# Gathers of two expert tables issued two and two instead of one and one, from expert 33 on

## The chip, the core and the metric

The kernel runs on one core of one Trainium2 chip. Its time is the device time of one execution in microseconds (us). Work is spread over five engines that run their own instruction streams and meet only at semaphores: TensorE (PE, matmuls), VectorE (DVE), ScalarE (ACT), GpSimd (POOL) and SyncE (SP). Transfers run on 16 DMA engines; GpSimd issues the ones that this case is about.

## The reference, cut to what matters

Two transformer blocks follow each other. The change lies in the expert layer of the first one, in which each of 256 tokens picks 8 x 16 = 128 experts out of 16384, and each expert is one row of 1024 numbers in each of two tables:

```
def expert_chunk(args):                      # 128 tokens a chunk
    xc, ic, gc = args
    u = jnp.take(u_tab, ic, axis=0)          # rows of the first table
    a = jnp.einsum('chkd,cd->chk', u, xc)    # one dot a token and expert
    wgt = gc * jax.nn.gelu(a)
    vv = jnp.take(v_tab, ic, axis=0)         # rows of the second table
    return jnp.einsum('chk,chkd->cd', wgt, vv)
```

## The kernel before

The 256 tokens are two tiles of 128; a token is a partition. "Expert e" in the code is one of 128 places of a tile: e from 0 to 127 is the first tile, 128 to 255 the second. For each e GpSimd issues one indirect DMA that fetches for each of 128 tokens its own row of the first table (`gather_u`, L687, 128 rows of 4 KB, 512 KB) and one of the second table (`gather_v`, L701, as large). So there are 512 gathers, which land in a buffer of 12 slots of 1024 numbers a partition: `NU` = 5 slots for the first table and `NV` = 7 for the second.

What uses them, in this order for each e:

- VectorE multiplies the row of the first table with the token and sums (L2489), and then counts the semaphore `dot_ready` up (L2491). Between these dots it also does pieces of the routing that finds the next experts.
- ScalarE makes the weight of the expert from the dot (L1737, L1741) and spreads it on a diagonal 128x128 matrix (L1746), of which there are 8 places.
- TensorE multiplies the diagonal with the row of the second table and adds to a sum in PSUM (L1143; two matmuls, which the profile shows as four records). After every odd e it counts `pair_summed` up. Between the sums it does matmuls of the next layers and of the routing (L780, L1069 and others), whose results ScalarE copies out of PSUM (L1563).

GpSimd's stream is written out by hand and is in order: an instruction that waits holds all behind it. `gather_u(e)` waits until the dot of e-5 is done, since it overwrites that slot. `gather_v(e)` waits until the pair that holds e-7 is summed: with pairs counted after odd e, an odd e asks for the sum of e-6, and the even e behind it asks for the same count again. So only odd e can really wait there. At a few e `gather_u` also waits for the routing's indices (`idx_ready`), at multiples of 32 in the part that the change touches. Before, the order is u(e+1), v(e), u(e+2), v(e+1) and so on. SyncE streams the weights of the later layers (2 MB a piece) over its own queue at the same time, in parts of this stage.

Of the kernel before, what the change touches and what calls it, by code (L numbers as in the profile page):

```python
# [27 lines left out]
TT = SEQ // P  # L28
# [44 lines left out]
ROUTE = 2 * TOPK  # L73
EXPERTS = HEADS * TOPK
# [170 lines left out]
def pairs(experts):  # L245

    return (experts + 1) // 2


def build(nc, T, out):  # L250

    with ExitStack() as ctx:
# [195 lines left out]
        def flag(name):  # L448

            if name not in S_:  # L450
                S_[name] = sem(name)
            return S_[name]

        def group_wait(eng, name, i):
            g = (name, i)
            eng.wait_ge(bank_full[GROUP_BANK[g]], GROUP_USE[g] + 1)
# [52 lines left out]
        def turn_wait(eng, *u):  # L509

            eng.wait_ge(turned, turn_no[u] + 1)
# [22 lines left out]
        def summed_wait(eng, t):  # L534

            eng.wait_ge(flag("pair_summed"), pairs(EXPERTS * (t + 1)))
# [5 lines left out]
        def route_step(e):  # L542

            return e // TOPK if e < ROUTE else e // ROUTE + 1
# [7 lines left out]
        def _(sp):  # L552
            second_halves = []
            for c, (_, w, k0, kt, col, n) in enumerate(CHUNKS):
                b = BEFORE[c]
                if c == FRONT:
# [79 lines left out]
        def _(pool):  # L636
# [41 lines left out]
            def gather_u(e):  # L678

                r, k, slot = e // ROUTE, e % ROUTE, e % NU  # L680
                if e in FIRST_IDX:
                    pool.wait_ge(flag("idx_ready"), FIRST_IDX.index(e) + 1)
                elif e == TOPK or (k == 0 and r):
                    pool.wait_ge(flag("idx_ready"), route_step(e) + len(FIRST_IDX))
                if e >= NU:
                    pool.wait_ge(flag("dot_ready"), e - NU + 1)
                pool.indirect_dma_start(  # L687
                    u_rows[:, slot, :], None, T["peer_u"],
                    bass.IndirectOffsetOnAxis(ap=expert_idx[:, r % 2, k:k + 1], axis=0),
                ).then_inc(u_full[slot], 16)  # L690

            def gather_v(e):

                r, k, slot = e // ROUTE, e % ROUTE, e % NV
                if e >= NV:
                    pool.wait_ge(flag("pair_summed"), pairs(e - NV + 1))
                if e == 0:
                    turn_wait(pool, "m", 1, 0)
                if e == 3:
                    group_wait(pool, "out1", 1)  # L700
                pool.indirect_dma_start(  # L701
                    v_rows[:, slot, :], None, T["peer_v"],
                    bass.IndirectOffsetOnAxis(ap=expert_idx[:, r % 2, k:k + 1], axis=0),
                ).then_inc(v_full[slot], 16)
# [1 line left out]
            gather_u(0)  # L706
            gather_v(0)
            gather_u(1)
            for e in range(1, TT * EXPERTS):
                if e + 1 < TT * EXPERTS:  # L710
                    gather_u(e + 1)
                gather_v(e)

            summed_wait(pool, TT - 1)
            pool.wait_ge(flag("dot_ready"), TT * EXPERTS)
# [2465 lines left out]
```

## Time and profile before

| | |
|---|---|
| median of 3 runs | 1384.9 us (1382.9 to 1387.51) |
| profiled execution, first to last instruction | 1366.9 us |
| first gather issued, last sum of experts | 152 us, 914 us |
| gathers | 512 of 512 KB |
| GpSimd busy | 500.2 us |

The profile gives the span of the profiled execution and not a time of its own that takes in what lies around it; median less span is 18.0 us, which is the start and the end of a run as far as this shows. Over half of the span is the expert stage. Its rows are read from GpSimd's timeline (when a gather is issued, and how long GpSimd sat idle before it), from the DMA share and rate in stretches of time, and from the count of matmuls that TensorE had begun by then. A gather's record on GpSimd is only the issue; the transfer runs later.

### The profile page before, as it was taken

Reading aid. Unit: us, or ns where it says so; the run is one execution under the profiler, and the core shown is the slowest. Engines: PE = TensorE matmul, PEld = TensorE weight load, DVE = VectorE, ACT = ScalarE, POOL = GpSimd, SP = SyncE. Lnnn points to the kernel's source line nnn. Section 1 sums busy time; section 2 is a strip of 40 time slices with the busy share of each in tenths; the row PEclk is TensorE's granted clock in tenths of the full one; section 3 lists DMA queues with packets and bytes.
Section 4 is the critical chain, followed back from the end, with each engine's and each line's share of the span. In section 5 each row is a group of like instructions: output and inputs, shape, how many; then the busy total and the mean of one; then the engine's idle time right before and its main releaser. Section 6 shows DMA issues by size and latency. Waiting matters only on the chain. (4 is left out here: it accounts for less than half of the span.)

```text
span 1366.9 us, 14592 instructions
## 1 busy us (share of the span) xinstructions
PE 1199.9 (88%) x4663; PEld 665.4 (49%) x4663; DVE 861.8 (63%) x1765; ACT 420.2 (31%) x1138; POOL 500.2 (37%) x580
## 2 busy tenths in 40 slices
PE   7899888888778978876788889789999999999997
PEld 4676554433344542222345433236544545999443
DVE  2657669574663654776746557679989543676345
ACT  2213334344223343343423324432323311222000
POOL 1000356666665666766666666630000000000000
PEclk9999999999998999999999999999999999999999
DMA  9998789999998999999999999986644444454450
GB/s 358 390 349 326 286 319 339 367 357 367 364 366 300 406 403 405 407 377 364 340 371 353 400 405 409 377 306 233 224 139 148 145 150 156 157 175 145 175 184 31
DMA packets 134303, 405.66 MB, mean 297 GB/s; under 512 B 10153, under 2 KB 11585, under 8 KB 133971
## 3 DMA queue, kind: packets, MB, share of 16 engines
q0 software_dynamic: 75024, 273.19, 53.1%
q1 hardware_dynamic: 57860, 127.48, 25.8%
q10 hardware_dynamic: 1342, 4.06, 0.8%
q8 instruction: 38, 0.62, 0.2%
q14 instruction: 39, 0.31, 0.1%
HBM read 403.12 MB, written 1.05 MB: 296 GB/s over the span
## 5 line engine op out<-in xcount | busy, mean ns | idle before, releaser
L1143 PE MATMUL psum<-gathered,modr 128*128 128x512 f32 x1024 | 505.0, 633 | 130.3 <-DMA gathered<-in_peer_v_dram,expert_idx 49.0
L2489 DVE CUSTOM_DVE_ANT_0 gathered<-gathered,psum 128x1024 f32<-128x1024 f32 x256 | 311.5, 1217 | 202.3 <-DMA gathered<-in_peer_u_dram,expert_idx 153.3
L1143 PEld LDWEIGHTS psum<-gathered,modr 128*128 128x128 f32 x1024 | 190.7, 199 | 404.7 <-issue 284.9
L687 POOL DMA_INDIRECT gathered<-in_peer_u_dram,expert_idx x256 | 244.9, 957 | 240.5 <-DVE expert_idx L1997 144.0
L701 POOL DMA_INDIRECT gathered<-in_peer_v_dram,expert_idx x256 | 242.6, 947 | 169.9 <-remote 73.7
L780 PE MATMUL psum<-featT,weight_ring 128*128 128x128 f32 (+2 forms) x960 | 145.3, 305 | 14.4 <-issue 11.3
L780 PEld LDWEIGHTS psum<-featT,weight_ring 128*128 128x128 f32 x960 | 133.7, 196 | 43.9 <-issue 35.6
L780 PE MATMUL psum<-weight_ring,featT 128*128 128x512 f32 x336 | 147.9, 596 | 1.3 <-ACT featT L1563 0.8
L1737 ACT ACTIVATE gel<-dots 128x1 f32<-128x1 f32 x256 | 51.1, 200 | 255.1 <-issue 128.1
L1746 ACT ACTIVATE modr<-ident,wgt 128x128 f32<-128x128 f32 x256 | 102.8, 402 | 18.5 <-issue 1.1
L780 PEld LDWEIGHTS psum<-weight_ring,featT 128*128 128x128 f32 x336 | 62.6, 190 | 78.8 <-issue 76.6
L1741 ACT ACTIVATE wgt<-gel,expert_gate 128x1 f32<-128x1 f32 x256 | 75.4, 294 | 17.9 <-issue 0.3
L1989 DVE TENSOR_TENSOR work<-work 128x1088 f32<-128x1088 f32 (+5 forms) x87 | 68.6, 801 | 9.6 <-issue 2.8
L725 POOL DMA_DIRECT2D gathered<-in_b_in_dram x6 | 5.3, 942 | 138.6 <-ACT gathered L1585 104.2
L1585 ACT COPY work<-psum 128x128 f32<-128x128 f32 x32 | 8.4, 262 | 81.5 <-remote 44.6
L1978 ACT ACTIVATE work<-work,pack 128x256 f32<-128x256 f32 x28 | 12.7, 500 | 56.8 <-DVE work L1989 56.8
L1989 DVE TENSOR_TENSOR vectors<-weight_ring 128x1024 f32<-128x1024 f32 x14 | 16.5, 1220 | 20.9 <-PE psum L1512 20.9
L1563 ACT COPY featT<-psum 128x512 f32<-128x512 f32 (+1 forms) x24 | 12.4, 554 | 55.0 <-PE psum L752 53.8
L780 PE MATMUL psum<-weight_ring,uT 128*128 128x512 f32 x64 | 28.2, 593 | 1.0 <-ACT gathered L1585 1.0
L1989 DVE TENSOR_TENSOR gathered<-gathered,psum 128x256 f32<-128x256 f32 (+1 forms) x17 | 8.6, 511 | 29.8 <-PE psum L780 24.9
L1473 PE MATMUL psum<-featT,weight_ring 128*128 128x128 f32 x224 | 27.3, 275 | 0.0
L1473 PEld LDWEIGHTS psum<-featT,weight_ring 128*128 128x128 f32 x224 | 26.1, 192 | 0.0
(443 smaller groups left out, 1343.1 us busy)
## 6 DMA issues: line engine op xcount, KB each, us to landing
weight_ring<-in_w_in_dram SPq DMA_DIRECT2D x16, 2048.0 KB
weight_ring<-in_w_up_dram SPq DMA_DIRECT2D x8, 2048.0 KB
weight_ring<-in_w_down_dram SPq DMA_DIRECT2D x8, 2048.0 KB
weight_ring<-in_ada_w_dram SPq DMA_DIRECT2D x5, 2048.0 KB
work<-in_ada_w_dram SPq DMA_DIRECT2D x5, 2048.0 KB, 16.3
weight_ring<-in_peer_wq_dram SPq DMA_DIRECT2D x3, 2048.0 KB
gathered<-in_ada_w_dram SPq DMA_DIRECT2D x2, 2048.0 KB, 14.5
gathered<-in_peer_u_dram,expert_idx POOLq DMA_INDIRECT x256
```

What stands on the lines that cost most here:

```text
L687: pool.indirect_dma_start(u_rows[:, slot, :], None, T["peer_u"], bass.IndirectOffsetOnAxis(ap=expert_idx[:, r % 2, k:k + 1], axis=0),).the ...
L701: pool.indirect_dma_start(v_rows[:, slot, :], None, T["peer_v"], bass.IndirectOffsetOnAxis(ap=expert_idx[:, r % 2, k:k + 1], axis=0),).the ...
L780: last = pe.matmul(psum[0:m, bank, 0:n], lhs(k), rhs(k), start=(k == 0), stop=(k == kt - 1))
L1143: mm = pe.matmul(psum[:, SUM_BANK + half, :], diag[:, e % 8, :], v_rows[:, slot, 512 * half:512 * (half + 1)], start=(e % EXPERTS == 0), s ...
L1473: last = pe.matmul(psum[:, UP_BANKS * (n % 2) + bank, at:at + P], a(g, m), b(g), start=(g == 0), stop=(g == 3))
L1563: ins = act.activation(dst, src, func, **kw) if func else act.copy(dst, src)
L1737: act.activation(gel[:, col:col + 1], dots[:, col:col + 1], ACT.Gelu_apprx_tanh)
L1741: act.activation(wgt[:, col:col + 1], gel[:, col:col + 1], ACT.Copy, scale=expert_gate[:, r % 2, k:k + 1])
L1746: act.activation(diag[:, e % 8, :], ident[:, :], ACT.Copy, scale=wgt[:, col:col + 1]).then_inc(flag("diag_full"), 1)
L1978: act.activation(ffT[:, k, :], ffT[:, k, :], ACT.Relu, bias=pk("b_up")[:, k:k + 1])
L1989: return dve.tensor_tensor(o, a, b, op)
L2489: dve.tensor_tensor_reduce(u_rows[:, slot, :], u_rows[:, slot, :], h2_rows[t], 1.0, 0.0, ALU.mult, ALU.add, dots[:, col:col + 1])
```

## The change

GpSimd's loop is left as it was up to e = 32. From e = 33 it goes in steps of two and issues u(e+1), u(e+2), v(e), v(e+1). The waits inside `gather_u` and `gather_v` and all other engines are untouched.

```
             gather_u(0)
             gather_v(0)
             gather_u(1)
-            for e in range(1, TT * EXPERTS):
-                if e + 1 < TT * EXPERTS:
-                    gather_u(e + 1)
+            for e in range(1, ROUTE + 1):
+                gather_u(e + 1)
                 gather_v(e)
+            for e in range(ROUTE + 1, TT * EXPERTS, 2):
+                for ahead in (e + 1, e + 2):
+                    if ahead < TT * EXPERTS:
+                        gather_u(ahead)
+                for now in (e, e + 1):
+                    if now < TT * EXPERTS:
+                        gather_v(now)
```

`ROUTE` is 32, `TT * EXPERTS` 256. On GpSimd, around the place where the new loop starts (the first row is u(32); u is L687 and v is L701), this stood before:

```order
L687 DMA gathered<-in_peer_u_dram,expert_idx 128x1024 [waits dot_ready,idx_ready]
L701 DMA gathered<-in_peer_v_dram,expert_idx 128x1024 [waits pair_summed]
L687 DMA gathered<-in_peer_u_dram,expert_idx 128x1024 [waits dot_ready]
L701 DMA gathered<-in_peer_v_dram,expert_idx 128x1024 [waits pair_summed]
L687 DMA gathered<-in_peer_u_dram,expert_idx 128x1024 [waits dot_ready]
L701 DMA gathered<-in_peer_v_dram,expert_idx 128x1024 [waits pair_summed]
L687 DMA gathered<-in_peer_u_dram,expert_idx 128x1024 [waits dot_ready]
L701 DMA gathered<-in_peer_v_dram,expert_idx 128x1024 [waits pair_summed]
```

And this stands there now:

```order
L687 DMA gathered<-in_peer_u_dram,expert_idx 128x1024 [waits dot_ready,idx_ready]
L701 DMA gathered<-in_peer_v_dram,expert_idx 128x1024 [waits pair_summed]
L687 DMA gathered<-in_peer_u_dram,expert_idx 128x1024 [waits dot_ready]
L701 DMA gathered<-in_peer_v_dram,expert_idx 128x1024 [waits pair_summed]
L687 DMA gathered<-in_peer_u_dram,expert_idx 128x1024 [waits dot_ready] x2
L701 DMA gathered<-in_peer_v_dram,expert_idx 128x1024 [waits pair_summed] x2
L687 DMA gathered<-in_peer_u_dram,expert_idx 128x1024 [waits dot_ready] x2
L701 DMA gathered<-in_peer_v_dram,expert_idx 128x1024 [waits pair_summed] x2
```

In each block of four only the two in the middle have changed places: u(e+2) stands one place earlier, ahead of v(e) with e odd, and v(e) one place later. This happens 111 times, for e = 33, 35, ... 253.

At the end of GpSimd's part of this stage (gathers of experts 254 and 255), this stood before:

```order
L701 DMA gathered<-in_peer_v_dram,expert_idx 128x1024 [waits pair_summed]
L687 DMA gathered<-in_peer_u_dram,expert_idx 128x1024 [waits dot_ready]
L701 DMA gathered<-in_peer_v_dram,expert_idx 128x1024 [waits pair_summed] x2
L718 DMA gathered<-xres 128x1024 [waits bank_free6,bank_free7,dot_ready,pair_summed]
```

And this stands there now:

```order
L687 DMA gathered<-in_peer_u_dram,expert_idx 128x1024 [waits dot_ready] x2
L701 DMA gathered<-in_peer_v_dram,expert_idx 128x1024 [waits pair_summed] x3
L724 DMA gathered<-xres 128x1024 [waits bank_free6,bank_free7,dot_ready,pair_summed]
```

The last gather of all is v(255) in both, in the same place.

## Rows read from the trace of the kernel before

**Rows 1.** The page: the span, and the whole of it in 40 equal slices

```profile
span 1366.9 us, 14592 instructions
...
DMA  9998789999998999999999999986644444454450
GB/s 358 390 349 326 286 319 339 367 357 367 364 366 300 406 403 405 407 377 364 340 371 353 400 405 409 377 306 233 224 139 148 145 150 156 157 175 145 175 184 31
```

**Rows 2.** The page: groups of the expert stage (busy, mean; idle before, what ended it)

```profile
L1143 PE MATMUL psum<-gathered,modr 128*128 128x512 f32 x1024 | 505.0, 633 | 130.3 <-DMA gathered<-in_peer_v_dram,expert_idx 49.0
L2489 DVE CUSTOM_DVE_ANT_0 gathered<-gathered,psum 128x1024 f32<-128x1024 f32 x256 | 311.5, 1217 | 202.3 <-DMA gathered<-in_peer_u_dram,expert_idx 153.3
...
L687 POOL DMA_INDIRECT gathered<-in_peer_u_dram,expert_idx x256 | 244.9, 957 | 240.5 <-DVE expert_idx L1997 144.0
L701 POOL DMA_INDIRECT gathered<-in_peer_v_dram,expert_idx x256 | 242.6, 947 | 169.9 <-remote 73.7
```

**Rows 3.** Stretches of 60 us (busy of PE, PEld, DVE, ACT, POOL; clock, DMA, GB/s)

```profile
320.00:380.00 60.00, 47.41 (x131) 21.90 (x132) 36.40 (x96) 20.19 (x68) 38.34 (x41) 0.94 0.97 362
...
500.00:560.00 60.00, 47.47 (x102) 17.49 (x103) 33.92 (x75) 22.17 (x70) 39.65 (x42) 0.97 1.03 406
```

**Rows 4.** GpSimd's timeline around one stop (start, length; idle before, releaser)

```profile
345.00 0.94 POOL L687 DMA_INDIRECT gathered<-in_peer_u_dram,expert_idx  x1 [0.30 <-issue]
349.51 0.94 POOL L701 DMA_INDIRECT gathered<-in_peer_v_dram,expert_idx  x1 [3.56 <-remote]
350.75 0.94 POOL L687 DMA_INDIRECT gathered<-in_peer_u_dram,expert_idx  x1 [0.30 <-issue]
```

**Rows 5.** GpSimd's timeline: the stop before and the stop behind that one

```profile
326.33 0.94 POOL L701 DMA_INDIRECT gathered<-in_peer_v_dram,expert_idx  x1 [3.23 <-remote]
...
372.63 0.94 POOL L701 DMA_INDIRECT gathered<-in_peer_v_dram,expert_idx  x1 [3.38 <-remote]
```

**Rows 6.** Stretches of 2 us, before and behind the stop at 349 us

```profile
344.00:346.00 2.00, 1.43 (x4) 0.49 (x3) 1.18 (x2) 0.62 (x3) 1.64 (x2) 1.00 1.04 422
...
350.00:352.00 2.00, 1.63 (x4) 0.68 (x4) 1.88 (x9) 0.77 (x3) 1.39 (x3) 1.00 0.66 156
```

**Rows 7.** Groups from 150 us to 345.9 (PE) and 345.98 (POOL)

```profile
L1143 PE MATMUL psum<-gathered,modr 128*128 128x512 f32 x250 | 125.0, 642 | 29.6 <-issue 17.0 <-ACT modr L1746 9.0 <-DMA gathered<-in_peer_v_dram,expert_idx 3.6
...
L701 POOL DMA_INDIRECT gathered<-in_peer_v_dram,expert_idx x65 | 62.3, 959 | 41.8 <-issue 16.2 <-remote 13.1 <-PE psum L1143 12.5
```

**Rows 8.** Timelines of TensorE and ScalarE at the stop at 326, TensorE before 349

```profile
322.18 1.05 PE L1069 MATMUL psum<-work 128*128 128x128 f32 x8
...
326.28 0.59 ACT L1563 COPY work<-psum 128x512 f32<-128x512 f32 x1 [4.90 <-remote]
...
338.32 3.81 PE L1143 MATMUL psum<-gathered,modr 128*128 128x512 f32 x8
```

**Rows 9.** Another stop: GpSimd's timeline, and groups from 150 to 457.3 us

```profile
456.34 0.94 POOL L687 DMA_INDIRECT gathered<-in_peer_u_dram,expert_idx  x1 [0.30 <-issue]
459.38 0.94 POOL L701 DMA_INDIRECT gathered<-in_peer_v_dram,expert_idx  x1 [2.10 <-remote]
...
L1143 PE MATMUL psum<-gathered,modr 128*128 128x512 f32 x384 | 191.5, 641 | 51.7 <-ACT modr L1746 23.6 <-issue 19.6 <-DMA gathered<-in_peer_v_dram,expert_idx 8.5
...
L701 POOL DMA_INDIRECT gathered<-in_peer_v_dram,expert_idx x101 | 96.3, 954 | 74.3 <-remote 27.8 <-issue 25.0 <-PE psum L1143 21.6
```

**Rows 10.** Waits before gathers, 254 to 906 us: L701 (two rows), L687 (one)

```profile
  remote: 70.4, 27
...
  PE psum L1143: 19.6, 8
...
  DVEq L2491: 17.7, 23
```

**Rows 11.** The chain that ended last: from the last gather's issue to its landing

```profile
904.90 7.71 DMA gathered<-in_peer_v_dram,expert_idx
```

**Rows 12.** GpSimd's timeline: a gather of the first table that waits

```profile
504.31 1.32 POOL L687 DMA_INDIRECT gathered<-in_peer_u_dram,expert_idx  x1 [1.90 <-DVEq L2491]
```

## The prediction

> **What bounds the kernel now.** I read the page first. The DMA share stands at 9 tenths or near it from the start of the expert stage to its end, and the rate in its slices moves between about 300 and 409 GB/s [rows 1]. The groups of the stage say the same from the side of the users: VectorE's dots stood idle mostly because a row of the first table had not landed (153.3 us), TensorE's sums because one of the second had not (49.0 us, the rest in weight loads) [rows 2]. So the stage is paced by gathers. Who paces the gathers differs by stretch, and that is the second view. From 500 to 560 us the share is 1.03 at 406 GB/s, the most that this stage shows for long: the transfers themselves are the bound. From 320 to 380 us it is 0.97 at 362 GB/s [rows 3]. Of the 19 slices that lie within the changed part (slices 8 to 26), 7 have 400 or more and 12 have less, 358.6 on average [rows 1]. Were those 12 raised to 405, they would give back 12 x 34.2 us x (1 - 358.6 / 405) = 47 us. That is a ceiling for anything that a better order of gathers can bring.
>
> What keeps the 12 lower is in GpSimd's timeline, the third view. Between stops it issues a gather each 1.24 us (0.94 and 0.30 behind it), which at 512 KB is 423 GB/s, more than the 409 of the best slice. Then, at a gather of the second table, it stops for 3.56 us [rows 4], and so it did 23.2 us earlier and does 23.1 us later, for 3.23 and 3.38 us [rows 5]: 16 gathers at 1.24 and one stop of 3.3, which is 8 experts in 23.2 us. The stop reaches the transfers: before it the share is 1.04 at 422 GB/s, right behind it 0.66 at 156 [rows 6].
>
> Why does it stop? The fourth view is a count. By 345.98 us GpSimd had issued 65 gathers of the second table, so the one that waits is v(65), which asks for the pair of experts 58 and 59. By 345.9 TensorE had begun 250 records of sums, at four an expert: experts 0 to 61 are done, and the one asked for lies in the row that ends at 342.1 [rows 7, 8]. The count was due 7 us or more before GpSimd saw it. ScalarE shows the same at the stop before: the scores that it copies were made by 323.23, and it is let go at 326.28, after 4.90 us of waiting, within 0.1 us of GpSimd [rows 5, 8]. So what TensorE has done comes late to whoever waits, and to several at once. At another stop, before v(101), the needed count is of experts 0 to 95; with 384 records begun by 457.28 their sums were only just made, and yet GpSimd waits only 2.10 us [rows 9]. Seen from TensorE's end the counts are late by over 7 us in one case and by about 2 in the other; seen from GpSimd's last issue (345.94, 457.28) they come 3.6 and 2.1 us later. The time since GpSimd fell still is what the cases share.
>
> **The change part by part.** Nothing is added or removed: 512 gathers, the same bytes, the same waits. In 111 blocks u(e+2) goes ahead of v(e), e odd, and each moves by one place, 1.24 us.
>
> - At a stop (v(e) waits, e odd): before, u(e+2) stood behind the wait; now it is issued first. There are 35 such stops in the changed part, 70.4 + 19.6 = 90.0 us in all, 2.6 each with the regular 0.30 in it [rows 10]. What this is worth hangs on what ends a stop. If it ends some time after GpSimd has fallen still, GpSimd now falls still 1.24 us later, the stop ends 1.24 us later and is as long as before: 16 gathers and 3.3 us for 8 experts, 23.2 us again, worth 0. If it ends at an instant that TensorE alone sets, the moved gather fills 1.24 us of it. I take the first, for what the two stops above share. The second is the lower bound in time, priced with the rivals.
> - Between stops: v(e) is issued 1.24 us later, lands later, and its sum is later by as much. But v(e+6), which asks for that sum, is moved back too (e+6 is odd). The loop of the second table has the same slack; v(e+1) keeps its place. Worth 0.
> - The first table: u(e+2) asks for the dot of e-3, now 9 issues behind that row's own gather (11.2 us) and not 10 (12.4). Where gathers land in some 7.7 us, as the last one does [rows 11], a dot of 1.22 us still ends before. Where weights share the engines it does not always: GpSimd waited for dots 23 times, 17.7 us in all [rows 10], as before u(117) for 1.90 us [rows 12]. These waits get longer for odd e and now hold up v(e) too. But there the share is 1.03 [rows 3], and the queue of issued gathers is what the engines work on; a later issue shortens the queue and not the rate. Worth 0 while it holds several gathers; the price without that cover is the second rival.
> - VectorE gets its rows two at a time, then none for two gathers. A dot is 1.22 us and the pace 2.9 us an expert [rows 2, 5], so the second of a pair waits no longer than it came early. Worth 0.
> - The end: v(255) keeps its place, and its landing is what the chain passes through [rows 11]. Worth 0.
>
> Sum: 0. The page's span stays at 1366.9 us, and with the 18.0 us by which the median exceeds it the time is 1384.9; I say 1384.
>
> Two rules of the Trainium skill bear on this. By "TensorE: Matmul & The Clock Gate" (The cost: per-tile semaphore tail) a matmul's increment is an event of tens of ns, about 25 + 26 ns for one; ScalarE's 3 us between the end of the scores and its release [rows 8] do not agree with it. By that rule a count would come at TensorE's instant, whatever GpSimd does, which is the second case of a stop, the first rival. The other speaks against any gain: "DMA: Bandwidth & Descriptors" (Where 436 GB/s comes from) has about 358 GB/s a core as what HBM gives. By it the 362 of 320 to 380 us would be the ceiling and the sum 0 for good; the 406 in the same stage [rows 3] does not agree, so I keep the 47 us as the ceiling.
>
> **The rivals.**
>
> 1. Faster: a stop ends at TensorE's instant, and each stop in a stretch below 400 GB/s is cut by 1.24 us. 12 of 19 slices have 35 x 12 / 19 = 22 stops: 27 us, 1358; with all 35, 43 us, 1342, which is close to the ceiling. For it: a semaphore has no reason to wait for GpSimd. Against it: the stops of 3.23, 3.56 and 3.38 us are nearly equal, though TensorE's work between them is not, and two waiters were let go together.
> 2. Slower: the wait of u(e+2) for a dot takes the place of the wait that is left. It sits in the stretches with weight traffic. The 23 waits, each 1.24 us longer, are 29 us, 1413, if nothing covers them; it decides when the queue of issued gathers runs dry, which by the 7.7 us from issue to landing [rows 11] takes a wait of about six gathers' issue. With a third of it uncovered, 1394.
> 3. The stops fall elsewhere. The order within a stop is new, so the counts that are seen at its end can be a pair more or a pair less, and a stretch can have a stop more or fewer. At 3.3 us each, two or three of them are 7 to 10 us to either side, 1375 to 1394.
>
> **How the numbers follow.** Unchanged cycle: 0.60, of which I give a bit over half to a time within 0.3% (4.2 us, about what this measurement can tell from no change), and the rest to both sides evenly by the third rival: 0.34 same, 0.13 faster, 0.13 slower. First rival 0.27, all faster. Second rival 0.13, all slower. So 0.40 faster, 0.34 same, 0.26 slower. The likeliest case has 1375 to 1394 for itself. The range reaches to the 1358 of the first rival, which leaves out the part of it beyond, and to 1397 on the other side, past the 1394 of the second.
>
> **What would show it.** Right: in the changed kernel's timeline stops before odd v stay 3.2 to 3.6 us long in the stretches below 400 GB/s, 8 experts keep to 23 us, and the last gather is issued near 905 us. First rival: stops of about 2.2 us, 8 experts in 22, the last issue near 878. Second: waits of L687 for VectorE's count well over 17.7 us, and a DMA share under 1.0 in the stretch 500 to 560. What would make the forecast wrong above all is that a stop is ended neither by GpSimd's stillness nor by TensorE, but by the queue of gathers itself: then one more gather in that queue could lengthen every stop, or one more count could slip through and remove some.

## The result, and the profile of the changed kernel

| | before | after |
|---|---|---|
| median, 20 executions each | 1380.5 us (1367.2 to 1387.5) | 1383.9 us (1378.7 to 1390.6) |
| profiled execution | span 1366.9 us [rows 1] | span 1380.0 us, its own time 1381.8 us |
| last gather issued | 904.90 us [rows 11] | 914.15 us |
| ratio after / before | | 1.0044, 95% interval 1.0023 to 1.0066 |

The change makes the kernel slower, by 0.44% or 6.1 us (0.0044 x 1380.5). The interval does not hold 1, though its lower end, 0.23%, lies under the 0.3% that this measurement can just tell from no change. The ratio compares only undisturbed executions taken beside each other on a chip, so it is not the quotient of the two medians. Of the executions of before, 8 of 20 are under 1376 us; of the changed kernel none is under 1378.7. The profile of before [rows 1] was one of those quick executions, so the 13.1 us between the two spans are not the price of the change.

The page of the changed kernel: span, DMA share and rate in 40 slices, the groups of the expert stage (all lines behind the loop are 6 higher).

```profile
span 1380.0 us, 14592 instructions
...
DMA  9999779999999999999999999986744534444450
GB/s 358 390 350 329 288 268 337 371 356 363 355 359 356 404 404 405 350 344 368 364 362 348 398 404 408 350 323 213 244 133 142 152 121 162 174 157 153 180 182 31
...
L1149 PE MATMUL psum<-gathered,modr 128*128 128x512 f32 x1024 | 513.0, 648 | 139.6 <-ACT modr L1752 65.8
L2495 DVE CUSTOM_DVE_ANT_0 gathered<-gathered,psum 128x1024 f32<-128x1024 f32 x256 | 311.0, 1215 | 201.5 <-DMA gathered<-in_peer_u_dram,expert_idx 151.6
...
L687 POOL DMA_INDIRECT gathered<-in_peer_u_dram,expert_idx x256 | 245.2, 958 | 246.6 <-DVE expert_idx L2003 143.8
L701 POOL DMA_INDIRECT gathered<-in_peer_v_dram,expert_idx x256 | 243.5, 951 | 171.8 <-remote 67.8
```

Against [rows 1] most slices move by a few GB/s in either direction, some by far more: the 13th has 356 where before had 300, the 6th, which ends ahead of the change, 268 where it had 319. Two neighbours fall together, the 17th and 18th (552 to 621 us): 350 and 344, where before had 407 and 377. And TensorE's sums, which had waited most for rows of the second table (49.0 us, [rows 2]), now wait most for ScalarE's diagonal (65.8 us).

The waits before gathers between 254 and 930 us, L701 (two rows) and L687 (one), in us and times. `remote` is a count that came when no instruction that sends it had just ended; `DVEq` is VectorE's count of dots:

```profile
  remote: 66.5, 27
...
  PE psum L1149: 23.7, 15
...
  DVEq L2497: 22.4, 21
```

At gathers of the second table GpSimd sat idle for 90.2 us, where it was 90.0 [rows 10]. The waits of the first table for a dot rose from 17.7 to 22.4 us. Three stops in GpSimd's timeline (start, length; idle before, releaser), with the gathers ahead of them:

```profile
369.68 0.94 POOL L687 DMA_INDIRECT gathered<-in_peer_u_dram,expert_idx  x1 [0.30 <-issue]
373.10 1.35 POOL L701 DMA_INDIRECT gathered<-in_peer_v_dram,expert_idx  x1 [2.48 <-remote]
...
387.20 0.94 POOL L687 DMA_INDIRECT gathered<-in_peer_u_dram,expert_idx  x1 [0.30 <-issue]
390.92 0.94 POOL L701 DMA_INDIRECT gathered<-in_peer_v_dram,expert_idx  x1 [2.77 <-PE psum L1149]
...
547.25 0.94 POOL L701 DMA_INDIRECT gathered<-in_peer_v_dram,expert_idx  x1 [2.23 <-remote]
```

The second gather of the pair is now issued ahead of the stop, and the stop is still 2.2 to 2.8 us here. That is less than the 3.2 to 3.6 us of [rows 4, 5], but before has such stops too (2.10 us in [rows 9]). Of all stops over 0.5 us from expert 33 on, the 67 in two profiles of before average 2.65 us, the 65 in two of the changed kernel 2.63 (the second profile of each belongs to the repeats below). Last, three stretches (busy of PE, PEld, DVE, ACT, POOL; clock, DMA share, GB/s) of after:

```profile
320.00:380.00 60.00, 51.84 (x161) 25.92 (x160) 37.55 (x94) 22.93 (x74) 39.04 (x42) 0.94 0.95 359
500.00:560.00 60.00, 46.45 (x91) 17.09 (x89) 27.50 (x57) 18.80 (x60) 35.63 (x38) 0.89 1.03 405
560.00:600.00 40.00, 32.06 (x67) 12.37 (x68) 30.98 (x82) 16.95 (x51) 26.72 (x28) 0.96 0.91 338
```

and the third of them in the kernel before:

```profile
560.00:600.00 40.00, 32.41 (x63) 12.20 (x62) 28.62 (x71) 16.95 (x51) 26.31 (x28) 0.87 0.99 379
```

The first two answer to [rows 3] and have hardly moved. The third is new to this document: the share falls from 0.99 to 0.91 and the rate from 379 to 338 GB/s.

### The profile page after: what moved, and what is told of

Same layout as the page of the kernel before. It is cut to its first block, busy times and chain, and to the rows that moved or that the text cites. A ratio compares the mean times of both kernels' runs of the same rounds, so it can differ in the third digit from the quotient of the medians.

```text
span 1380.0 us, 14592 instructions
## 1 busy us (share of the span) xinstructions
PE 1207.1 (87%) x4663; PEld 675.1 (49%) x4663; DVE 858.2 (62%) x1765; ACT 416.2 (30%) x1138; POOL 501.4 (36%) x580
## 4 chain that ended last, share of the span: by engine, by line
PE 43%; POOL 12%; issue 10%; DVE 9%; another core or an unknown queue 9%; DMA 8%; ACT 4%; DVEq 2%; ACTq 1%; POOLq 0%; SPq 0%
PE psum L786 18%; PE psum L1479 6%; POOL gathered L701 6%; PE psum L1518 6%; POOL gathered L687 6%; PE psum L1149 6%; DMA gathered<-in_peer_u_dram,expert_idx 5%; DVE gathered L2495 3%; ACT modr L1752 1%; DVEq L2497 1%; DMA work<-in_ada_w_dram 1%; DMA weight_ring<-in_w_in_dram 1%; DMA gathered<-in_peer_v_dram,expert_idx 1%; PE psum L879 1%
## 5 line engine op out<-in xcount | busy, mean ns | idle before, releaser
L1149 PE MATMUL psum<-gathered,modr 128*128 128x512 f32 x1024 | 513.0, 648 | 139.6 <-ACT modr L1752 65.8
L1149 PEld LDWEIGHTS psum<-gathered,modr 128*128 128x128 f32 x1024 | 201.1, 206 | 411.3 <-issue 354.0
L687 POOL DMA_INDIRECT gathered<-in_peer_u_dram,expert_idx x256 | 245.2, 958 | 246.6 <-DVE expert_idx L2003 143.8
L701 POOL DMA_INDIRECT gathered<-in_peer_v_dram,expert_idx x256 | 243.5, 951 | 171.8 <-remote 67.8
L1995 DVE TENSOR_TENSOR work<-work 128x1088 f32<-128x1088 f32 (+5 forms) x87 | 68.7, 803 | 12.2 <-issue 5.8
L1995 DVE TENSOR_TENSOR vectors<-weight_ring 128x1024 f32<-128x1024 f32 x14 | 16.5, 1219 | 20.9 <-PE psum L1518 20.9
L1995 DVE TENSOR_TENSOR gathered<-gathered,psum 128x256 f32<-128x256 f32 (+1 forms) x17 | 8.6, 511 | 29.8 <-PE psum L786 24.9
```

Of the source, the lines that this page charges most:

```text
L687: pool.indirect_dma_start(u_rows[:, slot, :], None, T["peer_u"], bass.IndirectOffsetOnAxis(ap=expert_idx[:, r % 2, k:k + 1], axis=0),).the ...
L701: pool.indirect_dma_start(v_rows[:, slot, :], None, T["peer_v"], bass.IndirectOffsetOnAxis(ap=expert_idx[:, r % 2, k:k + 1], axis=0),).the ...
L1149: mm = pe.matmul(psum[:, SUM_BANK + half, :], diag[:, e % 8, :], v_rows[:, slot, 512 * half:512 * (half + 1)], start=(e % EXPERTS == 0), s ...
L1995: return dve.tensor_tensor(o, a, b, op)
```

## The experiments

Two theories went in. Theory A: a stop ends some time after GpSimd has fallen still, whatever the order, and the loss comes from where the stops now fall. Theory B, the second rival of the prediction: a gather of the first table asks for its dot one place sooner, and that wait is the loss. Below, "asks n behind" means that a gather stands n issues behind the gather whose dot or sum it waits for; these counts come from the issue order, not from a trace. All ratios are to the kernel before, run beside the experiment.

**Where a pair begins.** The same pairs one expert later, from e = 34 (the edit is shown against the changed kernel), so that the gather which is moved past v(e) is another.

```
-            for e in range(1, ROUTE + 1):
+            for e in range(1, ROUTE + 2):
...
-            for e in range(ROUTE + 1, TT * EXPERTS, 2):
+            for e in range(ROUTE + 2, TT * EXPERTS, 2):
```

> The pairs begin at e = 34: v(e) with e even moves one place back, and it never asks for a new count; odd v and the waits of odd v keep their place, even u(e+2) asks for its dot one place sooner. Theory A (a stop at odd v ends some 3 us after GpSimd's last issue, and the loss comes from moving the gather that stops): stops at odd v as in the kernel before, 8 experts apart in the stretches below 400 GB/s, time that of before within 0.3%. Theory B (the loss comes from gathers of the first table that ask for a dot one place sooner): as slow as the changed kernel, +0.4%, with waits of L687 for VectorE over 20 us.

Measured: 1378.9 us, ratio 1.0016 (0.9989 to 1.0042). Not told apart from either kernel. GpSimd waited 24.5 us for dots and 96.6 us for sums (from 240 us on), so neither wait went away.

**One place sooner without pairs.** u(e+2) ahead of v(e), one and one.

```
-            for e in range(1, TT * EXPERTS):
-                if e + 1 < TT * EXPERTS:
-                    gather_u(e + 1)
+            for e in range(1, ROUTE + 1):
+                gather_u(e + 1)
+                gather_v(e)
+            gather_u(ROUTE + 2)
+            for e in range(ROUTE + 1, TT * EXPERTS):
+                if e + 2 < TT * EXPERTS:
+                    gather_u(e + 2)
                 gather_v(e)
```

> From expert 33 on one and one again, but every u(e+2) goes ahead of v(e): the move of the change for odd and even e alike. Theory A: the set of gathers at a stop is that of the changed kernel, so stops of about 2.9 us and 6 to 8 experts between them, +0.3 to +0.7%. Theory B: twice as many gathers ask sooner, so twice the loss, +0.8% or more, and waits of L687 for VectorE near 30 us.

Measured: 1380.6 us, 1.0023 (0.9996 to 1.0050). What was put there for theory B counted wrongly: one and one, every first-table gather still asks 10 behind, so this order does not double the demand. Only its place against the second table changes, which comes back below.

**Fewer buffers for the first table.** The order of before, `NU = 4`, `NV = 8`: every dot is asked for 8 behind.

```
-NU = 5
-NV = 7
+NU = 4
+NV = 8
```

> The order of before, with 4 slots for the first table and 8 for the second. The second table's gathers have one expert more of room before they stop, the first table's ask for a dot one expert sooner. Theory A: about 10 experts between stops of 3.3 us where it was 8, some 5 of 35 stops fewer, -15 to -20 us (-1.2%), unless the dot waits eat it. Theory B: dot waits rule, +1% or more, L687 waits for VectorE well over 40 us.

Measured: 1386.8 us, 1.0077 (1.0049 to 1.0105). Waits for dots 38.3 us, for sums 73.2 (from 240 us on). The 15 to 20 us that theory A hoped for did not come, and a shorter demand on dots costs by itself, with no pair anywhere.

**A throttle on the first table.** Five buffers, order of before, but each u(e) from e = 33 waits for the dot of e-3, 6 behind.

```
-                    pool.wait_ge(flag("dot_ready"), e - NU + 1)
+                    pool.wait_ge(flag("dot_ready"), e - NU + (3 if e > ROUTE else 1))
```

> The order of before; from expert 33 a gather of the first table waits for the dot of e-3 and not e-5, so that GpSimd can't run far ahead and is still for short times all along. Theory A: the counts come through in these short pauses, the stops at odd v vanish or fall under 1.5 us, and the time falls by 10 to 40 us in spite of the waits. Rival (counts come at an instant that TensorE sets, stillness or not): the stops stay and the new waits add to them, +20 us or more.

Measured: 1394.6 us, 1.0135 (1.0086 to 1.0184). The waits of L687, and then of L701, from 254 us on:

```profile
  DVEq L2491: 55.6, 39
...
  remote: 37.6, 17
...
  PE psum L1143: 19.1, 14
```

Theory A had this kernel 10 to 40 us faster, and it is slower. Waits for dots tripled and waits for sums fell from 90.0 to 56.7 us. So a part of such waits is only exchanged: when GpSimd stands before a dot, the late counts of sums come in meanwhile. 37.9 us more here and 33.3 us less there do not add up to the 19 us that were lost (0.0135 x 1380), so idle time of GpSimd is not lost time one for one.

**Both kernels again,** unchanged, as a measure of the spread.

> The kernel before, unchanged, as a second profiled execution and as a measure of what a comparison on one chip shows of no change: ratio 1.000 within 0.25%. Of GpSimd's idle time from expert 33 on, the first profile has 13 us before gathers of the first table and 81 us before those of the second, beyond the regular 0.30. If executions repeat, these stand again within 2 us each; if they do not, differences of some us between two profiles say nothing of a change.

> The changed kernel, unchanged, beside the same runs of before: +0.2 to +0.7%, as before. Theory A (stops at odd v last as long as before and only their places move): idle time before gathers of the second table as in the kernel before, 75 to 85 us. Theory B (the moved gathers of the first table wait for dots): idle time before gathers of the first table above that of before_again by 4 us or more, as 19 against 13 in the first profiles.

Measured: 0.9998 (0.9971 to 1.0026) and 1.0042 (1.0017 to 1.0067). The loss is real and repeats. The waits do so less well: after_again had 29.1 us for dots and 77.0 for sums, before_again 17.5 and 87.4. Differences of some us in the waits of one profile decide nothing alone.

**One and one around the change of tiles only** (e = 113 to 144), pairs elsewhere.

```
+            for e in range(33, 113, 2):
...
+            for e in range(113, 145):
...
+            for e in range(145, 256, 2):
```

> Pairs as in the changed kernel, but one and one for e from 113 to 144, where the second tile begins: there u(135) has to wait for the dot of 130, which waits until the first tile's sum is read, and in pairs v(133) and v(134) stand behind it. If the loss sits there (4.6 us of waiting at that place in the profile of the changed kernel, none in that of before): within 0.2% of before. If it is spread over the stage: 0.3% or more above it.

Measured: 1.0039 (1.0014 to 1.0063). Most of the loss stays, which is what was expected of a loss that is spread over the stage and not of one that sits at this place. Its profile says more, below.

**Threes,** three gathers of each table in turn: dots asked for 8, 11 and 11 behind.

```
+            for e in range(ROUTE + 1, TT * EXPERTS, 3):
+                for ahead in (e + 1, e + 2, e + 3):
...
+                for now in (e, e + 1, e + 2):
```

> Three and three in place of two and two: in a block the third gather of the first table asks for its dot 8 issues (10.0 us) behind that row's own gather, where pairs have 9 and one and one has 10. Theory B (dot waits): idle time before the first table's gathers 30 us or more, time +0.8% or more. Theory A (only the places of the stops): +0.2 to +0.6%, idle time before the first table's gathers as in pairs, near 20 us.

Measured: 1.0118 (1.0087 to 1.0150), nearly three times the loss of pairs. That makes threes the better probe of a place: the next three put them in parts of the stage only.

**Threes where dots were waited for** (e = 90 to 149 and 210 to 248), **threes elsewhere** (33 to 89 and 150 to 209), **threes at the end** (from 249), and **pairs with the last seven experts one and one.**

```
+            for e in range(90, 150, 3):
...
+            for e in range(210, 249, 3):
```

> Three first-table gathers and then three second-table ones, for experts 90 to 149 and 210 to 248 only; one and one elsewhere, the last seven experts included. In these stretches first-table gathers waited for dots in the traces so far (19.1 us in all with pairs, 25.8 with threes). All threes cost a ratio of 1.0118. Theory B (the earlier demand for a dot costs): 1.007 to 1.010. Theory A (only where the stops fall counts, which is as likely anywhere): about half of what all threes cost, 1.004 to 1.006. If the end costs most: 1.000 to 1.003.

```
+            for e in range(33, 90, 3):
...
+            for e in range(150, 210, 3):
```

> Threes for experts 33 to 89 and 150 to 209 only, where the traces so far show nearly no wait for a dot; one and one elsewhere. Theory B: 0.999 to 1.002. Theory A: 1.004 to 1.006.

```
+            for e in range(249, TT * EXPERTS, 3):
```

> Threes for experts 249 to 255 only. In the traces so far the sums that TensorE still had to do behind GpSimd's last gather took 11.3 us with threes, 9.6 with pairs and 8.4 to 8.8 with one and one. If the end costs only that: a ratio of 1.002 (2.5 to 2.9 us). If the end is what costs in threes: 1.006 or more. If it costs nothing: 1.000.

```
+            for e in range(33, 249, 2):
...
+            for e in range(249, 256):
```

> The pairs of the change for experts 33 to 248, one and one for the last seven. The change cost 1.0044. If the end takes about 1 us of it: 1.0035. If the end takes all: 1.000. If the end takes none: 1.0044.

Measured, in this order: 1.0100 (1.0060 to 1.0141), 1.0047 (1.0017 to 1.0076), 0.9995 (0.9967 to 1.0023), 1.0064 (1.0029 to 1.0099). The end costs nothing, in threes or pairs. The busy stretches cost about what theory B gave, the calm ones more than it gave and just what theory A gave. So B is right on where most of it is, and does not hold for all of it.

**Pairs that ask for nothing sooner.** Six buffers for each table, and TensorE counts every sum. In this setting every gather asks exactly 12 behind, in any of the three orders: pairs and threes still bunch two and three gathers, dots and sums, but no wait is nearer than with one and one. The lines that place the sixth slot among the twelve are left out of the edit.

```
-NU = 5
-NV = 7
+NU = 6
+NV = 6
...
-    return (experts + 1) // 2
+    return experts
...
-                if e % 2:
-                    mm.then_inc(flag("pair_summed"), 1)
+                mm.then_inc(flag("pair_summed"), 1)
```

> The order of the kernel before, with six row buffers for each table in place of five and seven, and TensorE counting every sum instead of every second. Now each gather of either table stands 12 issues behind the gather whose dot or sum it asks for (before: 10 for the first table, 12 and 14 in turn for the second). This is the base of the next two kernels. Dots should be waited for for under 4 us where it was 13, sums for somewhat more than the 81 us of before. The time: a ratio of 0.995 to 1.010.

```
+            for e in range(33, 256, 2):
```

> The pairs of the change on top of the six buffers. Counted out, all gathers still stand 12 issues behind the one they ask for: pairs bunch the gathers of a table and ask for nothing sooner (with five and seven buffers they asked for a dot 9 and 11 issues behind in turn). Theory B (the earlier demand for a dot costs): the same time as six_one, within 0.2%, and the waits for dots as in six_one. The rival (the bunching of two sums or two dots costs, whatever is asked): the pairs' 0.4% to 0.6% again, on top of six_one.

```
+            for e in range(33, TT * EXPERTS, 3):
```

> Three and three on top of the six buffers; all gathers again 12 issues behind what they ask for. Theory B: the time of six_one within 0.3%. The rival (bunching): some 1.2% over six_one, as three and three cost with five and seven buffers.

Measured: one and one 0.9946 (0.9923 to 0.9969), pairs 0.9936 (0.9910 to 0.9962), threes 0.9969 (0.9949 to 0.9988). On top of six buffers the pairs cost nothing (0.9936 / 0.9946 = 0.9990), and threes 0.23% in place of 1.18%. Bunching as such is not what costs. The waits of six_one (L687, then L701) and of six_pairs:

```profile
  DVEq L2490: 2.7, 9
...
  remote: 51.7, 21
  PE psum L1143: 50.9, 34
```

```profile
  DVEq L2497: 12.3, 22
...
  PE psum L1150: 56.0, 38
  remote: 38.4, 19
```

The pairs do raise the waits for dots (2.7 to 12.3 us; theory B had them equal, which was wrong), and those for sums fall by 8.2: an exchange, with nothing lost. All three beat both kernels; six_one and six_pairs are 0.5 to 0.6% faster than before (0.995 to 1.010 was expected of six_one).

**The demand brought back.** Six buffers, but a first-table gather waits for the dot of e-5, as with five: 10 behind one and one, 9 and 11 in pairs (the edit is shown against the six-buffer kernels). And five and seven buffers with every sum counted.

```
-                if e >= NU:
-                    pool.wait_ge(flag("dot_ready"), e - NU + 1)
+                if e >= 5:
+                    pool.wait_ge(flag("dot_ready"), e - 4)
```

> six_one with one line changed: a gather of the first table waits for the dot of e-5, as with five buffers, though it has a sixth. So it asks 10 issues behind again, and nothing else differs. This is the base of the next kernel. Theory B: waits for dots rise from 2.7 us towards the 17.5 of before, and the time by 0 to 0.3% over six_one (a ratio of 0.995 to 0.998 to before).

> six_pairs with the same line changed: the first gather of a pair asks for its dot 11 issues behind, the second 9, as in the change; sums are asked for 12 behind, as in six_pairs. Theory B (the dot asked for 9 behind is what costs): 0.3% to 0.7% slower than ask5_one and than six_pairs. The rival (with six buffers it was the second table's new spacing that made the pairs free, not the first table's): the time of ask5_one, within 0.2%.

```
-    return (experts + 1) // 2
+    return experts
...
-                if e % 2:
-                    mm.then_inc(flag("pair_summed"), 1)
+                mm.then_inc(flag("pair_summed"), 1)
```

> The kernel before (five and seven buffers, one and one) with TensorE counting every sum, so that a second-table gather asks for a sum 14 issues behind at every expert, where it was 12 and 14 in turn. If the counting is what gains in six_one: a ratio of 0.993 to 0.997. If the sixth buffer of the first table gains it: 0.999 to 1.001.

Measured: ask5_one 0.9999 (0.9965 to 1.0033), ask5_pairs 1.0027 (0.9998 to 1.0056), each_sum 1.0009 (0.9980 to 1.0038). One line that asks for dots two places sooner takes away all that the six buffers gained (0 to 0.3% over six_one was expected, and it is 0.5%), and each_sum gains nothing: the gain is the first table's slack. Against six_pairs the same line costs the pairs 0.9% (1.0027 / 0.9936 = 1.0092; the two were measured on different chips, each beside before). Pairs against one and one at this demand are 0.28% slower (1.0027 / 0.9999), with intervals that overlap, so theory B's 0.3 to 0.7% is not told apart here from nothing.

## Why the prediction went wrong

The predicted 1384 us and the measured median of 1383.9 agree by luck: the three times shown of before were among its slower ones. What was forecast was no change, and the change is a loss of 6 us.

**A stop (worth 0): right.** Stops keep their length on average (2.65 and 2.63 us) though a gather more is issued ahead of them; in all they are 90.2 us where they were 90.0. The first rival wanted 1.24 us less at each, 27 us or more in all, and falls. Theory A is right on this much; that its stops fall in worse places was not shown by any run. The Trainium skill's tens of ns for a matmul's increment, "TensorE: Matmul & The Clock Gate" (The cost: per-tile semaphore tail), on which that rival leaned, do not agree with this stage: ScalarE's copy below is let go 7.6 us behind its matmul. Not right was that 8 experts keep to 23 us: the first two stops shown above lie 6 experts and 17.8 us apart, as some do in before_again. Nor does the last gather keep to 905 us; it is issued at 914.15 us.

**Second table, VectorE's pairs, the end (worth 0 each):** the end was tried by itself and costs nothing (0.9995). For the bunching of dots and sums the six-buffer kernels show the same. The second table's loop was not tried by itself.

**The first table (worth 0): this step failed.** The prediction saw that u(e+2) asks for its dot 9 issues behind and not 10, and put it at nothing, since "the queue of issued gathers is what the engines work on", "worth 0 while it holds several gathers". From 500 to 560 us that holds: the share stays at 1.03. Right behind it does not. Over the stage the runs give the demand a price: 0.9946 with every dot asked for 12 behind, 1 at 10, 1.0044 at 9 and 11 in turn, 1.0077 at 8, 1.0135 at 6 (the buffers of the second table differ too in the first and the fourth). So the second rival is what came, at 6 us where its prices were 9 (a third uncovered) to 29, though the sign that was given for it, a share under 1.0 from 500 to 560 us, did not show.

The cover was judged by the 7.7 us from issue to landing at the end of the stage [rows 11], and this was too short for its middle. Where VectorE had waited for a row of the first table, the profile of before has a median of 11.3 us from the start of the gather's issue to the start of the dot over experts 90 to 135 (26 dots, 5.5 to 16.9 us), and 6.5 us over experts 33 to 89. Nine issues are 11.2 us.

In the two profiles of the changed kernel most of the loss lies at one place that the prediction did not look at. VectorE reads the finished sums of the first tile out of PSUM behind the second dot of the second tile (L1995, before L1989: `modr<-psum,modr`), and for that it waits until v(127) is summed. The dots of 130 and on stand behind the read. With five buffers u(135) is the first gather that needs such a dot. One and one it is issued 13 places behind v(127), in pairs 11. v(133), which asks for the sum of 127 itself, stands 12 behind in both: one and one ahead of u(135), in pairs behind it. This is that place in the second profile of the changed kernel, in the timelines of ScalarE, TensorE, VectorE and GpSimd:

```profile
558.01 0.59 ACT L1569 COPY vectors<-psum 128x512 f32<-128x512 f32 x1 [10.43 <-remote]
...
559.13 0.40 ACT L1752 ACTIVATE modr<-ident,wgt 128x128 f32<-128x128 f32 x1
...
560.06 0.40 ACT L1752 ACTIVATE modr<-ident,wgt 128x128 f32<-128x128 f32 x1
...
549.28 1.12 PE L1210 MATMUL psum<-vectors,ones 1*128 1x512 f32 x2
...
559.68 3.75 PE L1149 MATMUL psum<-gathered,modr 128*128 128x512 f32 x4 [6.63 <-ACT modr L1752]
563.36 2.07 PE L1210 MATMUL psum<-vectors,ones 1*128 1x512 f32 x2
565.36 3.78 PE L1149 MATMUL psum<-gathered,modr 128*128 128x512 f32 x4
...
569.18 1.29 DVE L1995 TENSOR_TENSOR modr<-psum,modr 128x512 f32<-128x512 f32 x2 [10.87 <-PE psum L1149]
570.39 1.21 DVE L2495 CUSTOM_DVE_ANT_0 gathered<-gathered,psum 128x1024 f32<-128x1024 f32 x1
...
555.58 0.94 POOL L687 DMA_INDIRECT gathered<-in_peer_u_dram,expert_idx  x1 [0.30 <-issue]
559.02 0.94 POOL L701 DMA_INDIRECT gathered<-in_peer_v_dram,expert_idx  x1 [2.50 <-remote]
...
561.51 0.94 POOL L687 DMA_INDIRECT gathered<-in_peer_u_dram,expert_idx  x1 [0.30 <-issue]
571.90 0.94 POOL L687 DMA_INDIRECT gathered<-in_peer_u_dram,expert_idx  x1 [9.45 <-DVEq L2497]
```

Read from the top, it is a chain. ScalarE's copy waits 10.43 us for a count of TensorE, whose matmul ended at 550.40, and is let go 7.6 us later, within a stop of GpSimd (it fell still at 556.52 and goes on at 559.02). Behind the copy stand two diagonals, for which TensorE's last two sums of the tile had waited. TensorE had stood still for 6.63 us, and then it was slow: the two sums took 3.75 and 3.78 us and the matmul between them 2.07. The last is done at 569.14. VectorE then reads (it had waited 10.87 us), does a dot, and only then GpSimd issues u(135), after 9.45 us in which nothing was issued.

The same three of TensorE in the profile of before, and the stretch of each kernel's three (the clock is the third number from the end; the changed kernel first):

```profile
545.43 1.96 PE L1143 MATMUL psum<-gathered,modr 128*128 128x512 f32 x4 [0.56 <-ACT modr L1746]
547.32 1.12 PE L1204 MATMUL psum<-vectors,ones 1*128 1x512 f32 x2
548.37 1.98 PE L1143 MATMUL psum<-gathered,modr 128*128 128x512 f32 x4
```

```profile
559.68:569.14 9.46, 9.46 (x10) 2.82 (x10) 0.00 (x0) 2.87 (x9) 2.17 (x3) 0.50 0.82 326
545.43:550.35 4.92, 4.92 (x10) 1.62 (x10) 3.49 (x10) 2.28 (x7) 3.70 (x5) 1.00 1.03 410
```

The granted clock was 0.50 in the changed kernel, the lower of TensorE's two levels (1.2 GHz), and 1.00 (2.4 GHz) in before, where TensorE had stood still for 0.56 us only. That is 4.5 us of the delay (9.46 - 4.92). In the first profile of the changed kernel VectorE and GpSimd show the same, shorter:

```profile
559.10 1.29 DVE L1995 TENSOR_TENSOR modr<-psum,modr 128x512 f32<-128x512 f32 x2 [6.70 <-PE psum L1149]
...
561.82 0.94 POOL L687 DMA_INDIRECT gathered<-in_peer_u_dram,expert_idx  x1 [4.62 <-DVEq L2497]
```

In the profile of before VectorE did not wait for the read at all, and GpSimd's nearest waits for dots are 1.08 and 2.07 us:

```profile
551.25 1.27 DVE L1989 TENSOR_TENSOR modr<-psum,modr 128x512 f32<-128x512 f32 x2
...
558.40 0.94 POOL L687 DMA_INDIRECT gathered<-in_peer_u_dram,expert_idx  x1 [1.08 <-DVEq L2491]
...
562.65 0.94 POOL L687 DMA_INDIRECT gathered<-in_peer_u_dram,expert_idx  x1 [2.07 <-DVEq L2491]
```

Every kernel of this study passes this place, so their profiles can be ordered by it. "Places" counts the issues from v(127) to the first gather that needs a dot behind the read. The next columns are VectorE's idle time before the read, the time from the issue of v(127) to the read, and that from the issue of v(128) to v(136), which are 16 issues (17 in trios, trios_busy and six_trios). The share and rate are those of 560 to 600 us.

| kernel | places | idle before the read, us | v(127) to the read, us | v(128) to v(136), us | DMA share, GB/s | ratio |
|---|---|---|---|---|---|---|
| six_one | 15 | 2.46 | 17.3 | 25.2 | 0.99, 382 | 0.9946 |
| six_pairs | 14 | none | 14.8 | 23.7 | 1.00, 383 | 0.9936 |
| six_trios | 14 | 4.41 | 16.1 | 24.7 | 1.00, 385 | 0.9969 |
| before, before_again | 13 | none, 3.62 | 14.5, 18.2 | 24.6, 24.6 | 0.99, 379; 0.98, 380 | 1 |
| trios_tail | 13 | 4.45 | 19.0 | 25.5 | 1.00, 380 | 0.9995 |
| ask5_one | 13 | none | 14.5 | 24.8 | 0.97, 372 | 0.9999 |
| each_sum | 13 | 2.19 | 16.8 | 23.2 | 1.00, 391 | 1.0009 |
| trios_calm | 13 | none | 14.5 | 24.7 | 1.00, 385 | 1.0047 |
| skip_boundary | 13 | 7.21 | 21.8 | 28.3 | 0.97, 370 | 1.0039 |
| even_start | 13 | 9.04 | 22.4 | 30.0 | 0.87, 315 | 1.0016 |
| ask5_pairs | 11 | 6.63 | 16.2 | 25.1 | 0.95, 355 | 1.0027 |
| after, after_again | 11 | 6.70, 10.87 | 18.9, 23.5 | 27.8, 32.5 | 0.91, 338; 0.83, 311 | 1.0044, 1.0042 |
| pairs_notail | 11 | 7.24 | 20.1 | 29.1 | 0.88, 333 | 1.0064 |
| two_ahead | 11 | 11.79 | 23.9 | 32.8 | 0.81, 300 | 1.0023 |
| nu4_nv8 | 11 | 5.06 | 17.1 | 26.0 | 0.94, 346 | 1.0077 |
| trios_busy | 10 | 7.30 | 14.4 | 25.8 | 0.93, 336 | 1.0100 |
| trios | 10 | 10.38 | 20.1 | 31.6 | 0.90, 334 | 1.0118 |
| throttle | 9 | 7.67 | 17.1 | 28.6 | 0.84, 310 | 1.0135 |

The stretch of the share is fixed while the place moves: v(128) to v(136) are issued from 539.3 to 563.9 us in before, and from 532.3 to 556.0, ahead of the stretch, in six_pairs. So the time from v(128) to v(136) says more than the share. Two things lengthen it. One is the places: where the read comes 19 us behind v(127), it is 25.5 us at 13 places (trios_tail) and 27.8 at 11 (after), which is nearly two issues of 1.24 us. The other is a late read. It comes 14.5 to 19.0 us behind v(127) in the six profiles with 13 places that have no pairs, and 18.9 and 23.5 in the changed kernel. A late read does not need pairs at the place. skip_boundary, one and one there, shows the chain too, in ScalarE, TensorE, VectorE and GpSimd:

```profile
544.32 0.59 ACT L1581 COPY vectors<-psum 128x512 f32<-128x512 f32 x1 [6.76 <-remote]
...
545.99 3.75 PE L1161 MATMUL psum<-gathered,modr 128*128 128x512 f32 x4 [4.50 <-ACT modr L1764]
...
551.67 3.47 PE L1161 MATMUL psum<-gathered,modr 128*128 128x512 f32 x4
...
555.18 1.29 DVE L2007 TENSOR_TENSOR modr<-psum,modr 128x512 f32<-128x512 f32 x2 [7.21 <-PE psum L1161]
...
555.41 0.94 POOL L701 DMA_INDIRECT gathered<-in_peer_v_dram,expert_idx  x1 [4.74 <-PE psum L1161]
```

Here GpSimd stops before v(133) for the sum of 127, and v(128) to v(136) take 28.3 us. even_start does the same (5.01 us before v(133)).

An estimate of the price: the five profiles of one and one with 13 places (before, before_again, ask5_one, each_sum, and trios_tail, whose threes come later) take 24.5 us on average from v(128) to v(136), the four of pairs at 11 places 28.6, from 25.1 to 32.5. That is 4.1 us, out of the 6.1.

**What is shown, and what is not.** Shown by runs: the loss repeats; it is not at the end; it grows as dots are asked for sooner and is gone when they are asked for later, with the bunching unchanged; and the demand alone, brought back, costs what the slack had gained. That most of the changed kernel's loss falls at the place behind the read is read from its two profiles: 3.2 and 7.8 us more there than in the two of before. Ahead of it, from v(33) to v(128), they took 279.6 and 287.3 us where before took 283.6 and 281.1, and behind it, to v(255), 344.9 and 339.7 where before took 341.0 and 341.2, which is the spread of single executions. The one run that took the pairs away from there, skip_boundary, kept the loss, and its profile has the place 3.7 us longer all the same, by a late read. So the two places are at most a part of the price, and why the read comes late in some profiles and not in others is open. No kernel moved the read. And the place does not hold the loss of every kernel: trios_calm passes it like before (24.7 us), ask5_pairs and nu4_nv8 lose 0.5 and 1.4 us there, and they cost 0.27 to 0.77%. Where that is lost stays open.

**A number that was wrong on the way.** "The 18.0 us by which the median exceeds" the span do not lie around it: the changed kernel's profiled execution took 1381.8 us for a span of 1380.0. Before's profile was merely of a quick execution.

## What to carry to other kernels

- A change of order in one queue is priced by what each wait now asks for, counted in issues, at every place where another engine's stream has a special step. In the changed kernel's profiles a nearer demand cost nothing that stands out over most of the stage, and 3.2 and 7.8 us at one place, where the dots stand behind a read of finished sums and that read came late.
- A gather's time to landing is taken from the stretch where its cover is needed, not from the end: here 11.3 us in one stretch, 6.5 in another, 7.7 at the end.
- A DMA share of 1.03 says that a wait is covered now, not right behind that stretch. Look at the slice after it.
- Where a buffer can be moved between two users, count the slack of both: one more for the first table and one less for the second gained 0.5% (with every sum counted, which alone gained nothing), more than any order did here.

## What the runs showed of the hardware that was not expected

- To ask later for a sum did not lessen the waiting. With every sum counted, each second-table gather asks 14 issues behind, where it was 12 and 14 in turn, and GpSimd still sat 93.0 us before them, now in 48 waits (before 90.0 in 35):

```profile
  remote: 56.7, 23
  PE psum L1143: 36.3, 25
```

- What TensorE had done was seen late by others while GpSimd issued gathers without pause, by ScalarE too: its copy above was let go 7.6 us behind its matmul, inside a stop of GpSimd. That a late count then holds up TensorE itself, through ScalarE's diagonals (65.8 us of waits on the page of the changed kernel), was not foreseen. Why the counts come late stays open.
- A late count is paid twice. TensorE stood still for 6.63 us over it, and the granted clock of the 9.46 us behind that was 0.50: two sums of an expert took 3.75 and 3.78 us, where they took 1.96 and 1.98 at a clock of 1.00.
